# Where sixteen pieces of the first layer's modulation are multiplied, and one bank for the attention's outputs

## What is computed

```python
for l in range(DEPTH):
    ml = (silu(c) @ w_mod[l] + b_mod[l]).reshape(b, 1, N_MOD, d)       # latent tokens
    mc = (silu(c_ctx) @ w_mod[l] + b_mod[l]).reshape(1, 1, N_MOD, d)   # context tokens
    hl = modulate(rms_norm(xl, norm1_g[l]), ml[:, :, 0], ml[:, :, 1])
    ...
    out_l, out_c = token_mixers(hl, hc, w_in[l], ...)
    xl = xl + ml[:, :, 2] * out_l
    hl2 = modulate(rms_norm(xl, norm2_g[l]), ml[:, :, 3], ml[:, :, 4])
    ...
    xl = xl + ml[:, :, 5] * f[:b * s].reshape(b, s, d)
```

## Time and profile before

| | us |
|---|---|
| median of 3 runs (1609.22 to 1611.38) | 1610.6 |
| the profiled execution, from its first to its last instruction (its span; no other time of it is given) | 1600.8 |
| between the two | 9.8 |
| projection tiles 2 to 12, with the pieces between them | 73.44 to 164.07 |
| attention of the first layer | 330.10 to 379.00 |
| TensorE busy, whole span | 1472.3 |

### The profile page before, as it was taken

How to read it: one execution, slowest core, us unless ns; L and a number is a source line. 1 busy time by engine, 2 the same in 40 slices (tenths; PEclk the granted TensorE clock), 3 DMA queues, 4 the chain that set the end, 5 groups by cost and what they waited for, 6 DMA issues and landing times.

```text
span 1600.8 us, 20143 instructions
## 1 busy us (share of the span) xinstructions
PE 1472.3 (92%) x8062; PEld 1073.3 (67%) x8062; DVE 883.7 (55%) x1259; ACT 634.6 (40%) x853; POOL 364.8 (23%) x196
## 2 busy tenths in 40 slices
PE   6898999989999998799999999899988998998887
PEld 2565778756777765678888874697868995343334
DVE  4721567686322326889999977664783565111112
ACT  2422221166222224477877864442264443111002
POOL 0322342310222220201010002373314670000000
PEclk9999999999999998899999999998999998999997
DMA  8547331201655572699999994152304766999993
GB/s 342 177 182 272 98 100 59 80 21 54 210 184 184 197 249 110 262 343 399 410 402 411 401 327 144 55 183 79 107 21 170 251 217 254 398 421 420 422 420 146
DMA packets 118190, 367.45 MB, mean 230 GB/s; under 512 B 7918, under 2 KB 73776, under 8 KB 87248
## 3 DMA queue, kind: packets, MB, share of 16 engines
q1 hardware_dynamic: 109296, 334.62, 55.7%
q0 software_dynamic: 8800, 31.53, 5.3%
HBM read 353.53 MB, written 12.58 MB: 229 GB/s over the span
## 4 chain that ended last, share of the span: by engine, by line
PE 39%; DVE 9%; DMA 9%; issue 2%; ACT 1%; POOL 0%; SPq 0%; DVEq 0%; PEldq 0%; ACTq 0%
PE bank L977 9%; PE bank L979 9%; PE bank L978 9%; DMA operands_plain<-in_w_up_e 6%; PE bank L1462 4%; DMA ring<-in_w_down_e 2%; PE bank L1501 2%; PE bank L1426 1%; PE bank L1412 1%; PE bank L1471 1%; PE bank L1187 1%; DVE mix L2323 0%; DVE mix L2384 0%; PE bank L961 0%; PE bank L1033 0%
## 5 line engine op out<-in xcount | busy, mean ns | idle before, releaser
L808 POOL TENSOR_TENSOR w_lo<-ring,w_hi 128x1024 fp32r<-128x1024 f32 x120 | 300.1, 2512 | 597.8 <-ACT w_hi L1787 597.7
L977 PE MATMUL bank<-h_hi,w_hi 128*128 128x512 f32 (+1 forms) x768 | 275.1, 358 | 12.2 <-DVE h_lo L2174 7.0
L978 PE MATMUL bank<-h_hi,w_lo 128*128 128x512 f32 (+1 forms) x768 | 264.4, 344 | 0.0
L979 PE MATMUL bank<-h_lo,w_hi 128*128 128x512 f32 (+1 forms) x768 | 264.3, 344 | 0.0
L977 PEld LDWEIGHTS bank<-h_hi,w_hi 128*128 128x128 f32 x768 | 147.6, 192 | 53.4 <-issue 21.0
L979 PEld LDWEIGHTS bank<-h_lo,w_hi 128*128 128x128 f32 x768 | 147.8, 192 | 17.1
L978 PEld LDWEIGHTS bank<-h_hi,w_lo 128*128 128x128 f32 x768 | 148.0, 193 | 16.5 <-issue 1.4
L1787 ACT ACTIVATE w_hi<-ring 128x1024 fp32r<-128x1024 f32 x120 | 125.6, 1054 | 72.2 <-DMA ring<-in_w_in 34.2
L977 PE MATMUL bank<-w_hi,h_hi 128*128 128x512 f32 (+1 forms) x384 | 140.2, 365 | 6.8 <-DVE h_lo L2693 3.1
L979 PE MATMUL bank<-w_lo,h_hi 128*128 128x512 f32 (+1 forms) x384 | 136.9, 357 | 0.0
L978 PE MATMUL bank<-w_hi,h_lo 128*128 128x512 f32 (+1 forms) x384 | 136.8, 356 | 0.0
(11 more groups left out here) (352 smaller groups left out, 2819.7 us busy)
## 6 DMA issues: line engine op xcount, KB each, us to landing
ring<-in_w_in SPq DMA_DIRECT2D x52, 1024.0 KB, 5.1
ring<-in_w_down_e SPq DMA_DIRECT2D x36, 1024.0 KB, 7.2
ring<-in_w_up_e SPq DMA_DIRECT2D x34, 1024.0 KB, 7.6
mix<-in_w_gate_e SPq DMA_DIRECT2D x32, 1024.0 KB, 7.2
operands_plain<-in_w_gate_e SPq DMA_DIRECT2D x29, 1024.0 KB, 23.0
ring<-in_w_mod SPq DMA_DIRECT2D x24, 1024.0 KB, 7.0
mix<-in_w_mod SPq DMA_DIRECT2D x24, 1024.0 KB, 5.0
mix<-in_w_up_e SPq DMA_DIRECT2D x22, 1024.0 KB, 23.5
```

The source lines that it names most:

```text
L808: pool.tensor_tensor(w_lo[:, slot], rview(raw, 8)[:, :, x * P:(x + 1) * P], w_hi[:, slot].bitcast(F32), ALU.subtract).then_inc(w_l, 1)
L977: first = mm(dst, stat[0], mov[0], start=start, stop=False)
L978: mm(dst, stat[1], mov[0], start=False, stop=False)
L979: return first, mm(dst, stat[0], mov[1], start=False, stop=stop)
```

## The change

The sixteen pieces of sets 1 and 2 are no longer multiplied between projection tiles but in the attention's units: `MOD_UNITS` says how many in each, ahead of the unit's transposes. Set 1 (eight pieces) is done in units 0 to 5, its transposes stand in unit 7; set 2 in units 9 to 14, its transposes in the merge. Both use bank 7, and the attention's outputs of the first layer all go to bank 6. In the ring's order the pieces stand behind the early chunks of the merge, now four instead of three, and ahead of the others. The warming matmuls of the first layer's attention are left out. VectorE's gains and half gates move to the merge (m = 3). The places that hold the copied rows move (`mrows`), and `mbank` has the layer as an argument; those hunks are left out here.

```diff
@@ -90,8 +90,8 @@
 GATE_C0 = 14
-MOD_AFTER = {g: p for p, g in enumerate((1, 3, 4, 6, 7, 8, 10, 11))}
-MOD_COLS = {8: 1, 12: 2}
+MOD_UNITS = {0: 3, 1: 1, 2: 1, 3: 1, 4: 1, 5: 1, 9: 2, 10: 1, 11: 1, 12: 1, 13: 1, 14: 2}
+MOD_COLS = 7
 PRE = [6, 3]
...
@@ -483,13 +482,17 @@
             return bank[4 + k // 2][:, k % 2 * SEQ:(k % 2 + 1) * SEQ]
-        def mbank(i):
-
-            return bank[5 + i % 2]
+        def mbank(l, i):
+
+            return bank[7 if l == 0 and i else 5 + i % 2]
         def norm_bank(inst):
             return bank[0 if inst in (2, 4) else 7]
+
+        def attended_in(l, v):
+
+            return 6 + v % 2 * l
         fbank = [[bank[i] for i in (2, 3, 4, x)] for x in (0, 5)]
...
@@ -529,10 +532,11 @@
             for g in range(2 * IN_C - AHEAD):
                 if g % 2 == 0:
                     order.append(("in", l, (g + AHEAD) // 2))
-                if l == 0 and g in MOD_AFTER:
-                    order += [("mod", l, DK + 2 * MOD_AFTER[g] + h) for h in range(2)]
-            first = sorted({merge_chunk(m) for m in range(PRE[l])})
-            order += [("merge", l, i) for i in first + [i for i in range(MERGE_C) if i not in first]]
+            first = sorted({merge_chunk(m) for m in range(PRE[l] + (AHEAD if l == 0 else 0))})
+            order += [("merge", l, i) for i in first]
+            if l == 0:
+                order += [("mod", l, k) for k in range(DK, 3 * DK)]
+            order += [("merge", l, i) for i in range(MERGE_C) if i not in first]
             order += [("out", l, i) for i in range(OUT_C)]
             assert len(order) == before_experts[l]
         assert len(order) == MOD_C + DEPTH * (IN_C + MERGE_C + OUT_C)
...
@@ -715,8 +719,8 @@
                 sp.dma_start(mod_next, a["w_mod"][1, k * P:(k + 1) * P, i * RW:(i + 1) * RW]).then_inc(s_lds, 16)
-            base = at_of[("merge", 0, 0)]
-            mod_behind = {base + 5: [0, 1], base + 6: [2], base + 8: [3], base + 9: [4, 5, 6],
+            base = at_of[("out", 0, 0)] - MERGE_C
+            mod_behind = {base + 4: [0, 1], base + 6: [2], base + 8: [3], base + 9: [4, 5, 6],
                           base + 11: [7], base + 12: [8, 9, 10], base + 14: [11], base + 15: [12, 13, 14],
                           base + 17: [15], base + 18: [16, 17, 18], base + 19: [19], base + 20: [20],
                           base + 21: [21, 22, 23]}
...
@@ -982,14 +986,17 @@
                 pe.wait_ge(m_ev[l], 3 * l + i + 1)
                 for x in range(4):
-                    rows = mrows_next[i] if l else mrow[:, i % 2]
-                    last = tp(mbank(i)[:, x * P:(x + 1) * P], rows[:, x * P:(x + 1) * P], ident)
+                    rows = mrows[l][i]
+                    last = tp(mbank(l, i)[:, x * P:(x + 1) * P], rows[:, x * P:(x + 1) * P], ident)
                 last.then_inc(m_co[l], 1)
             def mod(l, i, k):
                 if i == 2 and k == 0:
-                    pe.wait_ge(m_tk[l], 3 * l + 1)
+                    pe.wait_ge(m_tk[l], 2 + 2 * l)
+                if l == 0 and i == 1 and k == 0:
+
+                    pe.wait_ge(j_a[l], TAKEN)
                 if l:
                     pe.wait_ge(s_lds, transforms_to(0) + 16 * (DK * i + k + 1))
                     w = mod_next
...
@@ -998,7 +1005,7 @@
                     pe.wait_ge(ring_full[at % RS], full_at(at))
                     w = ring[:, at % RS]
                 for c in range(4):
-                    last = mm(mbank(i)[32 * c:32 * c + 32, :], csil[:, k, :], w[:, c * 512:(c + 1) * 512],
+                    last = mm(mbank(l, i)[32 * c:32 * c + 32, :], csil[:, k, :], w[:, c * 512:(c + 1) * 512],
                               start=k == 0, stop=k == DK - 1)
                 last.then_inc(m_us if l else ring_used, 1)
...
@@ -1155,14 +1162,8 @@
                         spectra_a(l, 1)
                     elif g == 2:
                         spectra_b(l, 1)
-                    if l == 0 and g in MOD_AFTER:
-                        i, k = divmod(2 * MOD_AFTER[g], DK)
-                        for h in range(2):
-                            mod(l, 1 + i, k + h)
-                    if l == 0 and g in MOD_COLS:
-                        mod_columns(l, MOD_COLS[g])
-
-                pe.wait_ge(m_tk[l], 3 * l + 3)
+
+                pe.wait_ge(m_tk[l], 5 * l + 1)
                 fill_steps(plan[0])
                 for c in range(BK):
                     pe.wait_ge(j_d[l], 12 + c + 1)
...
@@ -1215,6 +1216,15 @@
                 units = units_of[l]
                 U = len(units)
+                one_bank = 1 - l
+                mod_pieces = iter(range(2 * DK))
+
+                def mods_in_unit(v):
+                    if l == 0 and v == MOD_COLS:
+                        mod_columns(l, 1)
+                    for _ in range(MOD_UNITS.get(v, 0) if l == 0 else 0):
+                        i, k = divmod(next(mod_pieces), DK)
+                        mod(l, 1 + i, k)
                 def scores(v):
                     c, x, s = units[v]
...
@@ -1241,23 +1251,25 @@
                 def values(v):
                     c, x, s = units[v]
-                    if v >= 2:
-                        pe.wait_ge(a_o[l], v - 1)
+                    if v >= 2 - one_bank:
+                        pe.wait_ge(a_o[l], v - 1 + one_bank)
                     pe.wait_ge(a_ev[l], 2 * v + 2)
                     n = 4 if s == 0 else 2
                     for k in range(n):
                         for h in range(2):
                             col = (2 * c + h) * DH
-                            last = mm(bank[6 + v % 2][h * DH:(h + 1) * DH, 0:P], vtok[:, 4 - n + k, col:col + DH],
+                            last = mm(bank[attended_in(l, v)][h * DH:(h + 1) * DH, 0:P], vtok[:, 4 - n + k, col:col + DH],
                                       pT_s[:, v % 2, h, k, :], start=k == 0, stop=k == n - 1)
                     last.then_inc(a_pv[l], 1)
                 scores(0)
                 scores(1)
-                keep_busy(4, 3)
+                if l:
+                    keep_busy(4, 3)
                 for v in range(U + 1):
                     if v + 2 < U:
                         scores(v + 2)
+                    mods_in_unit(v)
                     if v < U:
                         transposes(v)
                     if v:
...
@@ -1309,6 +1321,8 @@
                                 gate(0, x, j_pe[l], w_u if x > PRE[l] else None)
                             if l == 0:
                                 next_mod(1)
+                        if l == 0 and n == 0 and m == 1:
+                            mod_columns(0, 2)
                         if n == 0 and m < BEHIND[l]:
                             branch(0, m, 2, w_u if m == 0 else ring_used if m == 4 else None)
                             if l == 0 and m == DK - 1:
...
@@ -1732,14 +1746,11 @@
                 if l:
                     act.wait_ge(m_us, DK * (i + 1))
-                    if i:
-                        act.wait_ge(m_co[l], 3 * l + i)
-                    A(mrows_next[i], mbank(i)[:, :], ACT.Copy).then_inc(m_ev[l], 1)
-                    return
-                act.wait_ge(ring_used, direct_to[at_of[("mod", l, DK * i + DK - 1)]])
-                if i == 2:
-                    act.wait_ge(m_co[l], 3 * l + 1)
-                A(mrow[:, i % 2, :], mbank(i)[:, :], ACT.Copy).then_inc(m_ev[l], 1)
+                else:
+                    act.wait_ge(ring_used, direct_to[at_of[("mod", l, DK * i + DK - 1)]])
+                if 3 * l + i > 2:
+                    act.wait_ge(m_co[l], 3 * l + i)
+                A(mrows[l][i], mbank(l, i)[:, :], ACT.Copy).then_inc(m_ev[l], 1)
             def filter_sin(l, i):
...
@@ -1814,8 +1825,6 @@
                         spectrum_a(l, 1)
                     elif g == 2:
                         spectrum_b(l, 1)
-                    if l == 0 and g in (7, 11):
-                        mod_rows(l, g // 7 if g == 7 else 2)
                 for g in range(12, 16):
                     lead_in(g + AHEAD)
...
@@ -1889,7 +1898,7 @@
                     c, x, s = units[v]
                     act.wait_ge(a_pv[l], v + 1)
                     col = s * SEQ + x * P
-                    A(qT[:, c, col:col + P], bank[6 + v % 2][:, 0:P], ACT.Copy).then_inc(a_o[l], 1)
+                    A(qT[:, c, col:col + P], bank[attended_in(l, v)][:, 0:P], ACT.Copy).then_inc(a_o[l], 1)
                 act.wait_ge(y_z[l], 2 * S * BK)
                 exps(0)
...
@@ -1900,6 +1909,8 @@
                         evac(v)
                     if v:
                         attended(v - 1)
+                    if l == 0 and v == MOD_COLS - 1:
+                        mod_rows(l, 1)
                 act.wait_ge(a_tr[l], 2 * U)
                 def parts_in(n):
...
@@ -1973,6 +1984,8 @@
                             lead_merged(m - 1)
                         if m == 1 and n < 2:
                             parts_in(n + 1)
+                        if l == 0 and n == 0 and m == 0:
```

(33 more changed lines are left out.)

## The result

The changed kernel takes 1596.3 us (median of 4 runs, 1593.2 to 1600.7) against 1611.0 (4 runs, 1609.2 to 1612.6): ratio 0.9921, interval 0.9902 to 0.9941, faster by 14.7 us. 1597.8 was forecast.

The account below looks back on a forecast made before the run. TensorE, busy 92% of the span, was taken as the bound. Terms -27.6 + 12.4 + 2.7 + 0.3 - 2.0 + 1.0 + 0.4 = -12.8 us on the 1600.8 span gave 1588.0, plus 9.8 to the median: 1597.8 us, range 1591 to 1604.

Parts of the forecast that it names:

- The projection: First layer's projection: without sixteen pieces, their waits and two sets of transposes, it saves 27.6 us.
- rival D: Projection does not shrink, because another feeder turns up behind the pieces and takes 10 us: 1608 to 1613, chance 0.05.
- The pieces in the attention: Attention: pieces and transposes add 15.8 us, 3.4 of it absorbed in TensorE's idle time, growth 12.4 us.
- Rival A: Attention: idle time filled in full and loads never late, better than the sum, -18.1 us, 1592.5; chance 0.12.
- The load: Attention: TensorE waits 2.7 us in unit 1 for the fourth piece's load, perhaps 0.3 in unit 14; together 2.7 us.
- Rival B: Attention: the ring of three sets the pace, pieces wait about 7 us with half clock behind; -3.5 us, 1607; chance 0.12.
- One bank: Attention outputs: products wait for ScalarE's copy of the unit before, only in the last unit, 0.3 us.
- The ring's order: Rotary step: earlier chunk splits TensorE's waits in two; first scores 1 us earlier and at full clock, 2 us less.
- The clock in unit 0: Attention's unit 0: without warming matmuls the three pieces may run at half clock, 1.0 us, bounds 0 and 4.
- The merge: Merge: ScalarE's copy, four transposes and VectorE's moved work cost 0.4 us; late branch weights nothing.
- Rival C: Attention units 0 to 5 and 9 to 14: TensorE's clock stays at 1.2 GHz, slower; units 0 to 5 alone give 1620; chance 0.04.
- The rule weighed against the change: Attention: frequent short idles between groups of matmuls make the clock swing and cost throughput; no size given.

Follow-up runs that it names:

- again_after: The changed kernel run again without an edit, for a second profile: 1594.4 us, ratio 0.9913.
- busy: The changed kernel with the three warming matmuls put back in the first layer's attention: 1595.7 us (one run).
- front3_gap: The changed kernel with unit 0's three pieces ahead of the third scores and unit 1's piece moved to unit 6: 1588.4 us, ratio 0.9879.
- narrow: The changed kernel with the sixteen pieces multiplied over 32 of 512 columns: 4697.0 us (routing overflows, only the stage is read), attention 55.8 us.
- order_only: The kernel before with only the early merge chunks in the ring's order changed, four instead of three: 1610.9 us (one run).
- late_split: front3_gap with GpSimd's two last splits held until VectorE's rotary step is done, pieces spread anew: 1586.5 us, ratio 0.9855.

## Why the prediction came out right, step by step

1. **The projection: 27.6 us forecast, 27.1 measured** (123.5 to 124.2 in the four traces with the pieces between the tiles, 96.4 or 96.5 in the six without). Right: nothing turned up behind the pieces, rival D is out. The same stretch in before, from the dft (66.3) to the pooling:

```profile
66.30:190.00 123.70, 116.34 (x550) 79.94 (x551) 44.33 (x73) 27.00 (x33) 36.12 (x15) 0.99 0.56 204
```

Of the 27.2 us between the two, 7.4 were idle time (the waits for the pieces' loads) and 19.8 TensorE's own work. The same pieces cost 15 to 16 us in the attention. This is where the change gains.

2. **The pieces in the attention: absorbed 3.4 us forecast, 3.4 measured**, and as argued: unit 8's wait stays (1.4 us in the waits above), the others are gone. TensorE's busy time grew by 13.48 us, which is 15.8 for pieces and transposes, less 2.84 of warming, plus 1.5 of half clock now, less 0.85 of it before (2.74 us at 0.69): 13.6. Rival A is out, because of the empty units and the load.

3. **The load: one wait of 2.7 us in unit 1 forecast; 2.74, 1.58 and 2.40 measured** (after, again_after, busy), and none in unit 14 (367.18). Right, and so is its ground, 6.1 us from a free slot to use (5.7 to 6.2). Rival B is out for the later units: with some 3.2 us per unit the ring of three keeps up.

4. **One bank: 0.3 us forecast, 0.38 measured**, at the last unit alone.

5. **The ring's order: 2.0 us forecast; about 1.9 in one half of the executions, 0.4 to 0.6 in the other.** This is the mis-sized term. The waits came apart as said, and the first scores run at full clock (0.8 us less in the attention, in each trace). But the sum of VectorE's loss stayed (1.71 + 1.71 against 3.59), so the start could come earlier only by not falling to half clock. With the same two waits of 1.7 us it does not in again_after, front3_gap and narrow (15.5 us each), and does in after, busy and order_only (16.8, 17.0, 17.0). The step named one outcome where there are two.

6. **The clock in unit 0: 1.0 us forecast, 1.5 to 1.7 measured**, and not only there: it falls either on the pieces of unit 0 or on the matmuls behind the load's wait. busy shows that the second is enough. This term was sized too small by half a microsecond or more.

7. **The merge: 0.4 us forecast, nothing measured.** To the first residual it is 194.2 and 194.3 us with both kernels, and 194.0 to 194.9 in all variants; nothing larger is hidden, and the branch weights cost nothing.

Steps 2, 3, 4 and 6 as forecast, with the first scores' clock from step 5, make 16.4 - 0.8 = 15.6 us of growth; 15.0 and 15.9 were measured. From the dft to the first residual it is 507.8 to 494.7 in the pair run on one chip, **13.1 us where 12.8 had been forecast**, and 506.6 to 497.3 in the first pair, 9.3; the mean is 11.2. The two pairs differ by 1.2 us in the rotary step (the clock), by 0.9 in the attention (the clock and the load), and by 1.9 between pooling and rotary step, where nothing is changed. Rival C is out: the granted clock of the attention is 0.97.

**The base was wrong.** The prediction set out from a span of 1600.8 and took 9.8 us around it. It is 2.0; the other 8 were the distance of one fast execution from the median. The forecast survived since it carried the difference to the median as a constant.

**The rule weighed against the change** (the Trainium skill, "TensorE: Matmul & The Clock Gate", section "A second HAM failure mode: psum-queue depth-cycling") did not decide: the single 1.4 us wait of a repeat leaves 1.00, and so did. It bears on the rotary step, where one wait of 1.7 us leaves full clock and the second, 3 us later, leaves it in three traces of six and is followed by half clock in the other three.

**What stays open.** The medians differ by 14.7 us, and by 14.8 to 15.3 when both were run again; the stages up to the first residual by 9 to 13. The rest, some 3 us, lies in stages that the change does not touch: the head, router to experts (42.6 or 42.7 in four of the five full traces of the change and its variants, 45.3 to 45.5 in three of the four of before and its variants), the gather, where the change is slower, and the second layer. Whether any of it is the change's doing was not settled. So that the forecast met the median within 1.5 us is in part luck: the stages of its own sum gave 11.2 us on the mean, not 12.8, and time that no step accounts for made up for it.

## What to carry to other kernels

Work moved into a bottleneck engine's idle time is worth the idle time behind it in the queue's order, not that of the stage: 3.4 of 5.5 us here. Put the first pieces where the engine is sure to wait (ahead of the third scores), and leave out the unit whose operand can't be there yet: the same 16 pieces cost 6 to 7 us less. When a change touches stages that can be marked off, compare stages over several executions; the whole of one profiled execution against another was off by over 12 us.

## What the runs showed of the hardware

The length of a short wait alone did not settle the clock behind it here. Waits of 1.68 and then 1.75 us were followed by half clock (order_only), 1.68 and 1.74 were not (again_after); 3.27 us was in again_after and was not in after. In after, again_after, busy and late_split the first units lost 1.4 us or more to it, not all at the same place.

VectorE's rotary instruction with both inputs in SBUF takes 0.42 us when GpSimd is idle and 2.0 to 2.4 beside a split. In the change, timelines of GpSimd and VectorE:

```profile
290.02 4.73 POOL L812 TENSOR_TENSOR w_lo<-ring,w_hi 128x1024 fp32r<-128x1024 f32 x2
...
295.50 2.36 POOL L812 TENSOR_TENSOR w_lo<-ring,w_hi 128x1024 fp32r<-128x1024 f32 x1 [0.75 <-ACT w_hi L1798]
```

```profile
292.61 2.42 DVE L2396 TENSOR_TENSOR mix<-mix 128x256 f32<-128x256 f32 x1
...
295.53 0.42 DVE L2395 TENSOR_TENSOR mix<-bank,mix 128x256 f32<-128x256 f32 x1
295.99 2.15 DVE L2396 TENSOR_TENSOR mix<-mix 128x256 f32<-128x256 f32 x1
```

The first and the last begin inside a split and end 0.3 us after it: 295.03 against 294.75, 298.14 against 297.86. They wait the split out. The one between, of the same size, lies inside a split too and takes 0.42 us: one of its inputs comes from PSUM (`bank`). The Trainium skill, "SBUF — State Buffer", section "Who interferes with whom", says that a VectorE instruction with two SBUF inputs and a GpSimd one that reads SBUF exclude each other for the whole instruction; the trace agrees, and with the splits held back no such instruction of the rotary step took over 0.43 us (late_split). Pulling the splits apart did not shorten that; only moving them did.
